# Second block of a two-block transformer kernel: the gates' projection with the weights standing still, and softmax rows scaled by VectorE

## The reference, cut to what matters

```python
p = h @ w_in
q = axial_rope(to_heads(p[..., OFF_B_Q:OFF_B_K]), rows_pos, cols_pos)
...
na_lat = neighbourhood_attention(q, k, v, kc, vc, na_rpb)
...
def context_attention(qc, kc, vc):
    s = jnp.einsum('bqhd,bchd->bhqc', qc * (hd ** -0.5), kc)
    p = jax.nn.softmax(s, axis=-1).astype(vc.dtype)
    return jnp.einsum('bhqc,bchd->bqhd', p, vc).reshape(B, Lc, H * hd)
...
yb = na_out * jax.nn.silu(p[..., OFF_B_G:OFF_C_U])
...
return jnp.concatenate([ya, yb, yc], axis=-1) @ w_out
```

## Time and profile before

| | us |
|---|---|
| three runs | 3296.44, 3298.0, 3299.87 |
| median | 3298.0 |
| the profiled execution, its span | 3296.4 |
| second block in that span | 1825 to 3296 |
| first layer: g stream ends, attention | 2413.6; 2440.5 to 2533.1 |
| second layer: g stream ends, attention | 3112.4; 3129.7 to 3191.1 |

### The profile page before, as it was taken

One profiled execution on the slowest core, in us unless ns is written; L12 is line 12 of the kernel. 1 busy time (PEld: TensorE's weight loads), 2 busy tenths in 40 slices (PEclk: granted clock), 3 DMA queues, 4 the chain that ended last, 5 costly groups with the idle time before them and its releaser, 6 DMA issues.

```text
span 3296.4 us, 40653 instructions
## 1 busy us (share of the span) xinstructions
PE 3250.2 (99%) x15142; PEld 2650.1 (80%) x15142; DVE 2271.8 (69%) x4132; ACT 1554.2 (47%) x2872; POOL 90.8 (3%) x174
## 2 busy tenths in 40 slices
PE   9999999999999999999999999999999999999998
PEld 7888888888888788888888788888866778888766
DVE  7888888877776788888877633557556437746666
ACT  6545454445665555445555422222256336522464
POOL 0000000000000000000000000000000000000000
PEclk9999999999999999999999999999999999999999
DMA  8888877776545888788877432333322236533525
GB/s 285 261 267 262 258 260 259 251 260 197 153 147 173 260 260 268 260 259 260 268 261 264 131 104 89 95 100 96 96 80 78 86 100 192 181 116 96 176 72 171
DMA packets 285316, 614.21 MB, mean 186 GB/s; under 512 B 18688, under 2 KB 21312, under 8 KB 283456
## 3 DMA queue, kind: packets, MB, share of 16 engines
q1 hardware_dynamic: 261792, 527.50, 50.0%
q0 software_dynamic: 21952, 80.69, 7.5%
q10 hardware_dynamic: 1376, 3.44, 0.3%
HBM read 605.26 MB, written 6.29 MB: 186 GB/s over the span
## 4 chain that ended last, share of the span: by engine, by line
PE 93%; ACT 2%; DVE 2%; DMA 1%; issue 1%; SPq 0%; ACTq 0%; DVEq 0%
PE acc L430 29%; PE acc L431 28%; PE acc L435 28%; PE tp L2434 1%; PE acc L2455 1%; PE acc L2420 1%; DMA raw<-ffn_w_gu 1%; PE tp L2393 1%; PE tp L2002 1%; ACT pr L1068 0%; PE cgw L2405 0%; DVE lo L425 0%; PE cgw L2155 0%; PE tp L1964 0%; ACT hi L421 0%
## 5 line engine op out<-in xcount | busy, mean ns | idle before, releaser
L421 ACT ACTIVATE hi<-raw 128x512 fp32r<-128x512 f32 x1808 | 1135.1, 632 | 1546.7 <-PE acc L435 1472.5
L425 DVE TENSOR_TENSOR lo<-raw,hi 128x512 fp32r<-128x512 f32 x1808 | 1208.3, 689 | 832.4 <-ACT hi L421 823.3
L430 PE MATMUL acc<-hi,hT_hi 128*128 128x512 f32 x1760 | 696.2, 396 | 9.3 <-DVE hT_lo L1227 4.9
L431 PE MATMUL acc<-hi,hT_lo 128*128 128x512 f32 x1760 | 685.4, 389 | 0.0
L430 PE MATMUL acc<-hi,h_hi 128*128 128x512 f32 x1696 | 670.9, 396 | 6.8 <-ACT hi L421 3.8
L431 PE MATMUL acc<-hi,h_lo 128*128 128x512 f32 x1696 | 662.0, 390 | 0.0
L435 PE MATMUL acc<-lo,h_hi 128*128 128x512 f32 x1696 | 533.9, 390 | 0.4 <-DVE lo L425 0.4
L435 PE MATMUL acc<-lo,hT_hi 128*128 128x512 f32 x1760 | 513.6, 389 | 0.0
L430 PEld LDWEIGHTS acc<-hi,hT_hi 128*128 128x128 f32 x1760 | 330.4, 188 | 87.9 <-DVE hT_lo L1227 8.9
L431 PEld LDWEIGHTS acc<-hi,hT_lo 128*128 128x128 f32 x1760 | 330.6, 188 | 69.1 <-issue 2.6
L435 PEld LDWEIGHTS acc<-lo,hT_hi 128*128 128x128 f32 x1760 | 330.5, 188 | 69.1
(11 more groups left out here) (283 smaller groups left out, 2155.9 us busy)
## 6 DMA issues: line engine op xcount, KB each, us to landing
raw<-ffn_w_gu SPq DMA_DIRECT2D x352, 512.0 KB, 5.8
raw<-w_in SPq DMA_DIRECT2D x280, 512.0 KB, 3.8
raw<-ffn_w_down SPq DMA_DIRECT2D x176, 512.0 KB, 5.4
mw<-wmt POOLq DMA_DIRECT2D x132, 512.0 KB, 5.6
raw<-w_out SPq DMA_DIRECT2D x96, 512.0 KB, 4.1
mw<-wmt SPq DMA_DIRECT2D x60, 512.0 KB, 5.9
ball<-rpbx SPq DMA_DIRECT2D x8, 768.0 KB, 9.8
x<-x_rest SPq DMA_DIRECT2D x2, 2048.0 KB, 7.8
```

Of the source, the lines that this page charges most:

```text
L421: act.activation(hi[:, g % RING, :], raw_piece(g), ACT.Copy).then_inc(S["hi_made"], 1)
L425: dve.tensor_tensor(lo[:, g % RING, :], raw_piece(g), hi[:, g % RING, :].bitcast(F32), ALU.subtract).then_inc(S["lo_made"], 1)
L430: pe.matmul(bank, act_hi, hi[:, slot, :], start=start, stop=False)
L431: pe.matmul(bank, act_lo, hi[:, slot, :], start=False, stop=False)
```

## The change

In the g stream of both layers the operands change sides. A slice of 128 x 128 of the weights' piece is loaded, and the tokens `hT` move: 512 columns in the first layer, 256 in the second. Each bank then holds 128 channels x all tokens, four banks per chunk, with 12 matmuls per piece in both layers (so far 12 of 512 columns, and 6 of 512). ACT evacuates the banks with Silu straight into a new tile `gT`, channels on partitions. DVE's copies of g, ACT's Silu over all gates and the semaphore `gates_made` go.

In attention the gates are no longer multiplied by 1/sum, nor turned, nor copied. In their place DVE multiplies the rows of probabilities by 1/sum (`na_norm`): two instructions of 128 x 512 for a latent group, four of 128 x 256 for a context group. They stand first in DVE's step g, for group g itself, and PE's turns wait for them (`pr_made`) and no longer for ACT's `p_made`. `na_out` is one multiply of `acc[2]` or `acc[3]`, in turn, with the block of `gT`.

```diff
-                [("q", 0, 2, 2), ("k", 2, 2, 4), ("v", 4, 2, 4), ("g", 6, 2, 2)]]
+                [("q", 0, 2, 2), ("k", 2, 2, 4), ("v", 4, 2, 4), ("g", 6, 2, 4)]]
...
 # ACT
+                ph = phases[f"s{ly}g"]
+                for c in range(2):
+                    for j in range(LOOK, 16 + LOOK):
+                        hi_piece(act, ph.pieces + 16 * c + j)
+                    for b in range(4):
+                        bank_done(act, ph, 4, c, b)
+                        act.activation(gT[:, 4 * c + b, 0:nt * P], g_bank(nt, b), ACT.Silu).then_inc(S["acc_taken"], 1)
...
-                act.activation(qkvg[:, 3, 0:nt], qkvg[:, 3, 0:nt], ACT.Silu).then_inc(S["gates_made"], 1)
...
 # DVE
+                    if nm_ == "g":
+                        for i in range(n_):
+                            for j in range(LOOK, 16 + LOOK):
+                                lo_piece(dve, phases[f"s{ly}g"].pieces + 16 * i + j)
+                                tap(i, j - LOOK)
+                        break
...
-                def na_gate(g):
+                def na_norm(g):
                     s, t = 2 * g % 4, kinds[2 * g % U][1]
                     n = 2 if t == 2 else 1
                     dve.wait_ge(S["p_made"], 16 + u0 + 2 * g + 2)
-                    wait(dve, "gr_made", v0 + g - 1)
+                    wait(dve, "pr_made", u0 + 2 * g - 2)
                     link(dve.reciprocal(rr4[:, s:s + 2, 0:n], sm4[:, s:s + 2, 0:n]))
-                    for k in range(n):
-                        gv = qkvg[:, 3, t + k, g // G * P:(g // G + 1) * P].rearrange("p (e d) -> p e d", d=NA_D)
-                        ins = dve.tensor_tensor(gv, gv, rr4[:, s:s + 2, k:k + 1].broadcast_to([P, 2, NA_D]), ALU.mult)
-                    ins.then_inc(S["gr_made"], 1)
+                    for e in range(2):
+                        for k in range(n):
+                            cols = slice(k * L, 2 * L if n == 1 else (k + 1) * L)
+                            ins = dve.tensor_scalar(pr[:, s + e, cols], pr[:, s + e, cols], rr4[:, s + e, k:k + 1], None,
+                                                    ALU.mult)
+                        ins.then_inc(S["pr_made"], 1)
 
                 def na_out(g):
...
-                    dve.tensor_copy(block, tok_tiles(acc[3][:, cols])).then_inc(S["gt_taken"], 1)
                     dve.wait_ge(S["o_done"], 12 + v0 + g + 1)
-                    dve.tensor_tensor(block, tok_tiles(acc[2][:, cols]), block, ALU.mult).then_inc(S["o_taken"], 1)
+                    dve.tensor_tensor(block, acc[2 + g % 2][:, 0:n * P], block, ALU.mult)\
+                       .then_inc(S["o_taken"], 1)
 
                 def step(g):
                     p = g // G
-                    na_gate(g - 1)
+                    if g < 8 * G:
+                        na_norm(g)
...
                 for u in range(4):
                     na_max(u)
+                na_norm(0)
...
 # PE
+            def turned_stream(ph, chunks, nt):
+                for c in range(chunks):
+                    p0 = ph.pieces + 16 * c
+                    def high_product(j, b):
+                        if j == 0:
+                            pe.wait_ge(S["acc_taken"], ph.taken + 4 * (c - 1) + b + 1)
+                        w = hi[:, (p0 + j) % RING, b * P:(b + 1) * P]
+                        for h in range(2):
+                            pe.matmul(g_bank(nt, b), w, hT[h][:, kt_of(j), 0:nt * P], start=(j == 0 and h == 0), stop=False)
...
                 def na_turn(u):
-                    pe.wait_ge(S["p_made"], 16 + u0 + u + 1)
+                    pe.wait_ge(S["pr_made"], u0 + u + 1)
...
-                    na_gate(g - 1)
                     na_values(g - 1)
```

More of the change, by code:

```diff
@@ L375, in head_rows, with g_bank @@
         def head_rows(nt, n):
[L377 to L382, removed]
+            return gT[:, kt_of(n) - 4, 0:nt * P]
+        def g_bank(nt, b):
+            return acc[b][:, 0:nt * P]
         def shared(p):
@@ L2073, in stream, with low_product @@
                                                      ph.taken + min(t + 1 - before, 0)))
+            def turned_stream(ph, chunks, nt):
[7 more added lines that the diff above has]
+                            pe.matmul(g_bank(nt, b), w, hT[h][:, kt_of(j), 0:nt * P], start=(j == 0 and h == 0), stop=False)
+                    def low_product(j, b):
+                        last = pe.matmul(g_bank(nt, b), lo[:, (p0 + j) % RING, b * P:(b + 1) * P],
+                                         hT[0][:, kt_of(j), 0:nt * P], start=False, stop=j == 15)
+                        if j == 15 and b < 3:
+                            last.then_inc(S["acc_done"], 1)
+                        if b == 3:
+                            last.then_inc(S["pieces_used"], 1)
+                    for j in range(16):
+                        if 0 < j < 15:
+                            pe.wait_ge(S["hi_made"], p0 + j + 1)
+                            for b in range(4):
+                                high_product(j, b)
+                            pe.wait_ge(S["lo_made"], p0 + j + 1)
+                            for b in range(4):
+                                low_product(j, b)
+                        else:
+                            pe.wait_ge(S["lo_made"], p0 + j + 1)
+                            for b in range(4):
+                                high_product(j, b)
+                                low_product(j, b)
             def stream2(ph, src, chunks, after, ready=None):
@@ L2435, in na_turn @@
                     ins.then_inc(S["pt_done"], 1)
-                def na_gate(g):
-                    t, c0 = kinds[2 * g % U][1], g % 2 * L
-                    pe.wait_ge(S["gr_made"], v0 + g + 1)
-                    pe.wait_ge(S["o_taken"], B_HEADS + v0 + max(g - 1, 0))
-                    for k in range(2 if t == 2 else 1):
-                        ins = pe.transpose(acc[3][:, c0 + k * P:c0 + (k + 1) * P],
-                                           qkvg[:, 3, t + k, g // G * P:(g // G + 1) * P], ident[:])
-                    ins.then_inc(S["gt_done"], 1)
                 def na_values(g):
-                    t, c0 = kinds[2 * g % U][1], g % 2 * L
+                    t = kinds[2 * g % U][1]
                     w, first, n = (P, 0, 4) if t < 2 else (L, 2, 2)
                     pe.wait_ge(S["pt_taken"], u0 + 2 * g + 2)
+                    pe.wait_ge(S["o_taken"], B_HEADS + v0 + max(g - 1, 0))
                     for j in range(n):
                         for e in range(2):
-                            ins = pe.matmul(acc[2][e * NA_D:(e + 1) * NA_D, c0:c0 + w],
+                            ins = pe.matmul(acc[2 + g % 2][e * NA_D:(e + 1) * NA_D, 0:w],
                                             qkvg[:, 2, first + j, pair_cols(0, g // G, e * NA_D, NA_D)],
```

30 lines of the change are left out of this document (12 added, 18 removed).

## The result

The changed kernel takes 3306.53 us (median of 7 runs, 3304.18 to 3309.35) against 3298.0 before (7 runs): ratio 1.0025, 95% interval 1.0016 to 1.0034, so +8.5 us. The profiled execution has a span of 3305.4 against 3296.4, +9.0. Eight more runs, beside 24 of before, gave 3305.67 against 3298.11, ratio 1.0026 (1.0016 to 1.0036). So it is slower by 0.25%, inside the predicted range of 3294 to 3309, outside the forecast's own range of 3296 to 3305, and more than twice the predicted difference of +3.5.

What follows compares the result with a forecast made beforehand. PE was taken as the bound, busy 99% of the span. Stream +1.3, first layer +1.6 and second -1.8 gave +1.1; with +1.7 for clock and +0.7 for hand-overs, +3.5: 3301.5 us, range 3294 to 3309 (8 in 10).

Steps and rivals of the forecast that it cites:

- rival (c): Attention's first groups, both layers: wait for scaled rows returns, low clock lasts two stretches longer in each; +7.9, 3306; chance 0.20.
- The gates' stream: Second layer: 256-column matmuls at 0.113 to 0.120 each; +1.3 us, bounds -0.9 and +2.6; first layer 0.
- Rival (a): Gates' stream: weight loads become visible, 0.11 each on 384 more matmuls, 42 us, some 3340; chance 0.04.
- The steady loop: First layer's attention: DVE to ACT to DVE loop of 11.39 per pair of heads against 11.19; +1.7 in the sum.
- The hidden gates' work: Silu over all gates and DVE's gate copies in the stream: removing them gains 0, since nobody on the chain waits.
- PE's own period: First layer's attention: PE's work per pair falls from 10.66 to 10.22 and does not set the period.
- rival (d): Attention, both layers: PE sets the period through sooner hand-overs; -6, or -7 with the stream's near end, about 3291; chance 0.08.
- The starts: Start of attention: first turn waits for maxima and scaling; +1.2 and +0.9 by layer, +1.7 more each if clock stays low.
- The first layer's end: Last exp's sum read to the output turns: 5.25 us falls to 3.9, so -1.3.
- The second layer's middle and end: Second layer's attention: PE still sets the period, 7.19 to 6.98 per pair, -1.5; end 4.95 to 3.7, -1.2.
- the plain sum of +1.1: Stream +1.3, first layer +1.6, second layer -1.8, with the clock as in the kernel before.
- The 2.4 that the forecast had added for the clock and loose hand-overs: Starts of attention: +1.7 for low clock, as likely as not in each layer, and +0.7 for one more loose hand-over.

## Why the prediction was right in its direction and range, and short in its middle

The direction was right and the range held; the forecast's own range (3296 to 3305) did not. The measured 3306.5 is the time that rival (c) gave, 3306 to 3307, but not for its reason: it stood on two further stretches at half clock at each start, and the profiled execution has none there. That the two agree is luck.

- **The gates' stream** was priced +1.3 between -0.9 and +2.6; it is +2.55. The mechanism was right, the value taken wrong: the excess over the pure columns belongs to every matmul, not to every column. The row of 0.111 for 128 columns drew the estimate down; the run with 128 columns shows that it is a floor and no point on that line. Rival (a) is out: loads of 0.19 disappear at a pitch of 0.120 too. The Trainium skill ("TensorE: Matmul & The Clock Gate", Part 3: Packing small matmuls) lists as what overlaps that a load overlaps a matmul in flight only on another row group (a sentence before it also allows for a background weight buffer); the windows here, with loads and matmuls both busy for 46.05 of 46.05 us on full rows, don't bear the first out.
- **The steady loop**, 11.39 summed and 11.44 measured, is the step that was right in kind and size; leaving out, splitting and doubling the passes all move it as a loop does. The hidden gates' work (Silu, copies) was worth nothing, as said: from the convolution's turns to the first maximum it is 25.20 and 15.62 before and after.
- **PE's own period** in the first layer was put at 10.22, from the mean of a long window. In a steady pair of before PE is busy for 10.86 of 11.19; less the four turns of gates that is 10.43, and 10.42 was measured without the scaling passes. One wait of 0.44 for ACT's evacuation comes on top. So 10.86 is the least that was reached, in three of the runs. This didn't touch the forecast, but rival (d) counted on 0.43 per pair where 0.33 was to be had.
- **The starts** were summed at +1.2 and +0.9, with +1.7 as the case of a second stretch at half clock. They are +1.88 and +2.07 without a second stretch in the profiled execution. The way to the first turn was right: 2.0 later by the sum, 1.77 and 2.09 measured. The step that failed is what was taken off again, some 0.8 to 1.1, because turns and staging would run on a clock that is back by 2446. The stretch moved with the first turn (in the first layer from 2.1 to 4.0 us after the first maximum), and turns and staging together took no less than before (1.94 and 1.62 us, 1.97 and 1.49 before). A longer stretch, as in rival (c), was seen in other executions: 6.9 us at the first layer's start in the second profile of the change, 10.3 at the second's in the run with 128 columns.
- **The first layer's end** was to save 1.3 and cost 0.28. The sum of steps was right (6.80 with the clock held is 1.34 less than 8.14). What was missing: I had counted the new wait of PE at the starts against the clock, and not the same wait of 1.94 at the end, where half clock took 1.62 in this execution and nothing in the second profile of the change.
- **The second layer's middle and end** went the way that was summed: the period fell by 0.20 (0.21 summed), the middle by 0.96 of 1.5, and the end is -1.26 (of -1.2).

So the plain sum of +1.1 became +6.65: 1.25 more in the stream, 1.85 at the starts, 1.6 at one end, 0.9 in the middles. The 2.4 that the forecast had added for the clock and loose hand-overs covered less than half of that.

## What to carry to other kernels

Work that hides beside other engines can become the bound when it is moved between two hand-overs of a loop: sum the loop in start-to-start times, and look at what is queued ahead of each step on its engine (here a multiply that waits for PE stood before a scaling that did not need it). When weights are made to stand still, the columns that move per load must stay wide: 512 columns cost 0.227, 256 cost 0.120, 128 cost 0.111. A new wait of PE costs itself, and it can cost a stretch at half clock on the work after it too, as at the first layer's end (1.6 us in one profile, none in another). Where such a stretch stood before, as at the starts, do not count on the delay to outlast it: it can move along. A few idle matmuls in the wait went with a held clock at most of these places; they must end with the wait, since each that runs past it costs its own length.

## What the runs showed of the hardware

- Matmuls of 128 columns, each with its own load of 128 x 128, followed each other at 0.111 us on the mean; 256 columns at 0.120, 512 at 0.227.
- Behind waits of 1.9 to 2 us PE often ran at half clock (0.50 granted, the 1.2 GHz level) for 3.4 us at a time, in some executions 6.9 or 10.3, which takes 1.7 us of PE's time per 3.4. It began up to several us after the wait, and not after every such wait; in one execution of the same kernel it came at an end of a stage and in another it did not. In the changed kernel the clock came back at 2450.2, after 3 us in which PE did nothing but transposes. The Trainium skill (the same page, Part 4: PE-mode transpose) has it that transposes do not count as busy PE for the clock in the usual way; the stretch here doesn't bear that out.
